# A new opening for a two-layer hybrid decoder: x and the first weights in alternating parts, low-rank sums out unscaled, squares later, and narrow even projections

## The reference, cut to what matters

```python
def rms_norm(x, g, eps=EPS):
    y = x * lax.rsqrt(jnp.mean(x * x, axis=-1, keepdims=True) + eps)
    return y * g

h = rms_norm(x, attn_norm_g[0])          # x: (1, 256, 2048)
p = h @ even_w_in[0]                     # 2048 -> 6304 columns
qa, ka, va = jnp.split(p[..., :3072], 3, axis=-1)
a_out = diff_attention(qa, ka, va, ...)  # 8 heads
b_out = rwkv7_time_mix(p[..., 3072:], ...)  # r, k, v (1024 each), 160 low-rank columns
x = x + concatenate([a_out, b_out]) @ even_w_out[0]
x = x + swiglu(rms_norm(x, ffn_norm_g[0]))
...                                      # layer 1: hgrn2 and its swiglu, then the final norm

# in rwkv7_time_mix: a mix of each token with the one before it, then
xm = p + (prev - p) * mu
w_log = -jax.nn.softplus(-(w0 + jnp.tanh(wl) @ w_up)) - 0.5     # wl, al, gl: the low-rank columns
```

## Time and profile before

| | |
|---|---|
| three runs, median | 2703.5 us (2700.93 to 2703.85) |
| the profiled execution's own time | 2699.04 us |
| its span | 2697.3 us |
| granted clock, mean | 0.991 |
| PE busy | 2589.8 us, 96% |
| DVE busy | 1933.1 us, 72% |
| ACT busy | 1268.1 us, 47% |
| POOL busy | 433.9 us, 16% |
| DMA, mean | 162 GB/s |

### The profile page before, as it was taken

One profiled execution on the slowest core, in us unless ns is written; L12 is line 12 of the kernel. 1 busy time (PEld: TensorE's weight loads), 2 busy tenths in 40 slices (PEclk: granted clock), 3 DMA queues, 4 the chain that ended last, 5 costly groups with the idle time before them and its releaser, 6 DMA issues.

```text
span 2697.3 us, 46875 instructions
## 1 busy us (share of the span) xinstructions
PE 2589.8 (96%) x16654; PEld 2254.0 (84%) x16654; DVE 1933.1 (72%) x2981; ACT 1268.1 (47%) x1721; POOL 433.9 (16%) x426
## 2 busy tenths in 40 slices
PE   7988888889999999999999999998999999999998
PEld 6777777778888888888888888887888888888886
DVE  6676676677666566656698999997666656665666
ACT  5444343445554344434465656564455434433444
POOL 1222222211110011101111212211121001100112
PEclk9999999999999999999999999998999999999999
DMA  6222222225455555555464444443455555555543
GB/s 251 93 99 97 89 96 96 88 87 188 173 188 191 189 188 189 189 187 187 167 205 158 156 158 159 165 156 140 172 189 188 192 187 189 190 189 187 187 164 133
DMA packets 65716, 437.89 MB, mean 162 GB/s; under 512 B 9424, under 2 KB 10832, under 8 KB 16848
## 3 DMA queue, kind: packets, MB, share of 16 engines
q1 hardware_dynamic: 61776, 435.84, 45.4%
q10 hardware_dynamic: 3840, 0.70, 0.1%
HBM read 434.41 MB, written 2.10 MB: 162 GB/s over the span
## 4 chain that ended last, share of the span: by engine, by line
PE 86%; DVE 8%; issue 3%; ACT 2%; DMA 0%; DVEq 0%; ACTq 0%; SPq 0%; POOL 0%; POOLq 0%
PE acc L338 52%; PE acc L343 27%; PE mixer_banks L1555 2%; DVE w_low L307 1%; PE mixer_banks L1272 1%; PE acc L319 1%; ACT w_high L302 1%; PE mixer_banks L1372 1%; PE mixer_banks L1359 1%; ACT arena L638 0%; DVE arena L362 0%; PE mixer_banks L1374 0%; DVE arena L972 0%; DVE arena L960 0%; DVE arena L899 0%
## 5 line engine op out<-in xcount | busy, mean ns | idle before, releaser
L307 DVE TENSOR_TENSOR w_low<-w_raw,w_high 128x1024 fp32r<-128x1024 f32 x838 | 1056.1, 1261 | 417.7 <-ACT w_high L302 407.0
L302 ACT ACTIVATE w_high<-w_raw 128x1024 fp32r<-128x1024 f32 x838 | 883.1, 1059 | 947.0 <-PE acc L343 927.7
L338 PE MATMUL acc<-h_split,w_high 128*128 128x512 f32 x4576 | 1194.9, 398 | 8.5 <-DVE arena L362 8.4
L338 PEld LDWEIGHTS acc<-h_split,w_high 128*128 128x128 f32 x4576 | 817.2, 190 | 161.7 <-issue 18.9
L343 PEld LDWEIGHTS acc<-h_split,w_low 128*128 128x128 f32 x4576 | 642.0, 190 | 55.7
L343 PE MATMUL acc<-h_split,w_low 128*128 128x256 f32 x4576 | 659.7, 282 | 0.0
L464 POOL TENSOR_TENSOR arena<-arena,norm_scale 128x256 f32<-128x256 f32 x202 | 218.6, 1082 | 1787.7 <-DVE arena L362 1786.5
L338 PE MATMUL acc<-mix_split,w_high 128*128 128x512 f32 x1876 | 480.4, 395 | 1.1 <-DVE arena L362 0.6
L338 PEld LDWEIGHTS acc<-mix_split,w_high 128*128 128x128 f32 x1876 | 336.4, 189 | 62.8 <-issue 3.6
L343 PEld LDWEIGHTS acc<-mix_split,w_low 128*128 128x128 f32 x1876 | 260.6, 190 | 21.3
L343 PE MATMUL acc<-mix_split,w_low 128*128 128x256 f32 x1876 | 266.8, 282 | 0.0
(11 more groups left out here) (253 smaller groups left out, 1640.7 us busy)
## 6 DMA issues: line engine op xcount, KB each, us to landing
w_raw<-w_gu SPq DMA_DIRECT2D x176, 1024.0 KB, 4.8
w_raw<-w_down SPq DMA_DIRECT2D x64, 1024.0 KB, 4.9
w_raw<-w_odd SPq DMA_DIRECT2D x64, 1024.0 KB, 4.8
w_raw<-w_even SPq DMA_DIRECT2D x50, 1024.0 KB, 4.9
w_raw<-w_down SPq DMA_DIRECT2D x32, 768.0 KB, 4.2
w_raw<-w_odd_out SPq DMA_DIRECT2D x16, 1024.0 KB, 4.8
w_raw<-w_even_out SPq DMA_DIRECT2D x10, 1024.0 KB, 4.9
w_raw<-w_even_out SPq DMA_DIRECT2D x6, 896.0 KB, 4.5
```

The source lines that it names most:

```text
L302: act.activation(wh[:, self.res, ks], raw[:, self.raw, ks], ACT.Copy).then_inc(high_done, 1)
L307: dve.tensor_tensor(wl[:, self.res, ks], raw[:, self.raw, ks], wh[:, self.res, ks].bitcast(F32), ALU.subtract).then_inc(low_done, 1)
L338: pe.matmul(acc[self.acc][:, 0:2 * T], wh[:, self.res, k], flat(split[:, src(k)]), start=k == 0, stop=k == self.kt - 1)
```

## The change

The diff does these things:

- SyncE loads block 0 in two halves, with the second quarter of x between them.
- ScalarE: quarter 0 of x, first half of block 0, quarter 1, second half, quarters 2 and 3, block 1, half of the squares, block 2, the other half, blocks 3 and 4, then the norm, block 5, and then the low-rank functions. VectorE follows the same order; its squares' tree stands behind block 2 and within block 3.
- The low-rank sums (blocks 0 and 1) leave PSUM unscaled (`raw_sum`), before the norm's scale is known; VectorE scales them later.
- TensorE's norm matmul stands in the middle of block 3, where it stood in the middle of block 1.
- "Narrow": in blocks 0 to 49 `w_high` multiplies the two parts in two matmuls of 256 columns that add up in the same 256 PSUM columns. The evacuation is then one product of those 256 columns with `nrs` on VectorE; GpSimd scales nothing in the even layer, and its consumers wait for `evac_done`.

```diff
-        used[0] = 0
+        used[0] = BEHIND_SHIFTS          # the squares lie behind r3 ... b_sum
         sq_all = take(KT, T)
...
+            def high_products(self, pe, k, both, stop):
+
+                if self.narrow:
+                    for c in range(2):
+                        pe.matmul(acc[self.acc][:, 0:T], wh[:, self.res, k], both[:, c], start=k == 0 and c == 0, stop=False,
+                                  skip_group_check=True)
+                else:
+                    pe.matmul(acc[self.acc][:, 0:2 * T], wh[:, self.res, k], flat(both), start=k == 0, stop=stop)
...
             def evacuate(self, dve, dst):
 
                 self.result(dve)
+                if self.narrow:
+                    dve.tensor_tensor(dst, acc[self.acc][:, 0:T], nrs, ALU.mult).then_inc(evac_done, 1)
+                    return
                 dve.reduce_sum(dst, acc[self.acc].rearrange("p (s t) -> p t s", s=2), AX.X).then_inc(evac_done, 1)
...
-            return lambda u: Block(EVEN + 6 * j + 6 + u, i, 12)
+            return lambda u: Block(EVEN + 6 * j + 6 + u, i, 12, narrow=True)
... SyncE
             load_x(0)
-            Block(LOWRANK).load(sp, w_even[LOWRANK])
-            for q in range(1, 4):
+            sp.wait_ge(low_done, 2)
+            sp.dma_start(raw[:, 0, 0:HALF], w_even[LOWRANK][:, 0:HALF]).then_inc(S["first_half"], 16)
+            load_x(1)
+            sp.dma_start(raw[:, 0, HALF:KT], w_even[LOWRANK][:, HALF:KT]).then_inc(landed[0], 16)
+            for q in range(2, 4):
                 load_x(q)
... GpSimd
-                scale_next(-1)
-                pool.wait_ge(S["even_scaled"], 6 * j + 7)
+                pool.wait_ge(evac_done, 6 * j + 9)
...
-                scale_next(0)
...
-                    if l in (2, 4):
-                        scale_next(l // 2)
...
-                scale_next(3)
-                scale_next(4)
...
-            scale(LOWRANK, r3[:, 0, 1:], "even_scaled")
-            scale(LOWRANK + 1, r3[:, 1, 1:], "even_scaled")
-            for u in range(5):
-                scale(EVEN + u, even_dst[u], "even_scaled")
... ScalarE
-            for half in range(2):
-                Block(LOWRANK).high(act, half)
             for q in range(4):
                 act.wait_ge(S[f"x_in{q}"], 16)
                 for k in range(4 * q, 4 * q + 4):
                     high_part(k, gn[:, G_ATT0 + k:G_ATT0 + k + 1])
+                if q == 0:
+                    act.wait_ge(S["first_half"], 16)
+                    act.activation(wh[:, 0, 0:HALF], raw[:, 0, 0:HALF], ACT.Copy).then_inc(high_done, 1)
+                if q == 1:
+                    Block(LOWRANK).high(act, 1)
...
             for half in range(2):
                 Block(LOWRANK + 1).high(act, half)
-            for q in range(4):
-                act.activation(sq_all[:, 4 * q:4 * q + 4], x[:, 4 * q:4 * q + 4], ACT.Square).then_inc(S["sq"], 4)
+            squares((0, 1))
+            for half in range(2):
+                Block(LOWRANK + 2).high(act, half)
+            squares((2, 3))
+            for n in range(LOWRANK + 3, LOWRANK + 5):
+                for half in range(2):
+                    Block(n).high(act, half)
+            norm(0)
+            for half in range(2):
+                Block(LOWRANK + 5).high(act, half)
... VectorE
+            def raw_sum(n, dst):
+
+                Block(LOWRANK + n, narrow=True).result(dve)
+                dve.tensor_scalar(dst, acc[n][:, 0:T], 1.0, None, ALU.mult).then_inc(evac_done, 1)
...
+            for half in range(2):
+                Block(LOWRANK + 1).low(dve, half)
+            raw_sum(0, r3[:, low_home[0], 1:])
+            for half in range(2):
+                Block(LOWRANK + 2).low(dve, half)
+            raw_sum(1, r3[:, low_home[1], 1:])
             dve.wait_ge(S["sq"], KT)
             dve.tensor_tensor(sq_all[:, 0:8], sq_all[:, 0:8], sq_all[:, 8:16], ALU.add).then_inc(S["sq_sum"], 8)
+            Block(LOWRANK + 3).low(dve, 0)
...
+            Block(LOWRANK + 3).low(dve, 1)
+            for half in range(2):
+                Block(LOWRANK + 4).low(dve, half)
...
+            dve.wait_ge(S["norm_rstd"], 1)
+            Block(EVEN, narrow=True).evacuate(dve, even_dst[0])
...
+            for n in range(2):
+                home = r3[:, low_home[n]]
+                dve.tensor_tensor(home[:, 1:], home[:, 1:], nrs, ALU.mult).then_inc(S["dve_once"], 1)
+                dve.wait_ge(S["dve_once"], 2 * n + 3)
+                dve.tensor_tensor(d3[:, n], home[:, 0:T], home[:, 1:], ALU.subtract).then_inc(S["dve_once"], 1)
+                dve.wait_ge(S["dve_once"], 2 * n + 4)
+                dve.scalar_tensor_tensor(xm[:, n], d3[:, n], gn[:, G_MUW + n:G_MUW + n + 1], home[:, 1:],
+                                         ALU.mult, ALU.add).then_inc(S["low_mixed"], 1)
+            Block(EVEN + 1, narrow=True).evacuate(dve, even_dst[1])
... TensorE
-            norm(0)
-            for n in range(LOWRANK + 2, EVEN + 6):
-                for half in range(2):
-                    Block(n).products(pe, half, hs)
+            for k in range(KT):
+                pe.wait_ge(S["h_low"], k + 1)
+                Block(LOWRANK, narrow=True).tile(pe, k, hs)
+            for n in range(LOWRANK + 1, EVEN + 6):
+                Block(n, narrow=True).products(pe, 0, hs)
+                if n == LOWRANK + 3:
+                    pe.wait_ge(S["sq_sum"], KT + 1)
+                    pe.matmul(bank(0)[:, 0:T], ones, nss, start=True, stop=True).then_inc(S["sq_total"], 1)
+                Block(n, narrow=True).products(pe, 1, hs)
...
-                pe.wait_ge(S["even_scaled"], 6 * j + 7)
+                pe.wait_ge(evac_done, 6 * j + 9)
                 pe.matmul(bank(3), rot, flat(aqk), start=True, stop=True).then_inc(S["at_rot"], 1)
```

More of the change, by code:

```diff
@@ L141, in build @@
         b_sum = take(2, P + 1)
+        BEHIND_SHIFTS = used[0]
         e1 = take(2, P + 1)
@@ L281, in build, with __init__ @@
         class Block:
-            def __init__(self, base, i=None, step=0, kt=KT):
-                self.kt = kt
+            def __init__(self, base, i=None, step=0, kt=KT, narrow=False):
+                self.kt, self.narrow = kt, narrow
                 self.n = base if i is None else base + step * i
@@ L318, in tile @@
                 stop = k == self.kt - 1
-                pe.matmul(acc[self.acc][:, 0:2 * T], wh[:, self.res, k], flat(split[:, k]), start=k == 0, stop=stop)
+                self.high_products(pe, k, split[:, k], stop)
                 last = pe.matmul(acc[self.acc][:, 0:T], wl[:, self.res, k], split[:, k, 0], start=False, stop=stop,
@@ L337, in run @@
                 for k in ks:
-                    pe.matmul(acc[self.acc][:, 0:2 * T], wh[:, self.res, k], flat(split[:, src(k)]), start=k == 0, stop=k == self.kt - 1)
+                    self.high_products(pe, k, split[:, src(k)], k == self.kt - 1)
                 if begins:
@@ L565, in _, with squares @@
                     high_part(k, gn[:, G_ATT0 + k:G_ATT0 + k + 1])
+                if q == 0:
[3 more added lines that the diff above has]
+                    Block(LOWRANK).high(act, 1)
+            def squares(qs):
+                for q in qs:
+                    act.activation(sq_all[:, 4 * q:4 * q + 4], x[:, 4 * q:4 * q + 4], ACT.Square).then_inc(S["sq"], 4)
             for half in range(2):
                 Block(LOWRANK + 1).high(act, half)
-            for q in range(4):
-                act.activation(sq_all[:, 4 * q:4 * q + 4], x[:, 4 * q:4 * q + 4], ACT.Square).then_inc(S["sq"], 4)
+            squares((0, 1))
[8 more added lines that the diff above has]
+                Block(LOWRANK + 5).high(act, half)
             act.wait_ge(S["lam_dve"], 3)
             act.activation(lamt[:, 2:4], lamt[:, 0:2], ACT.Exp).then_inc(S["lam_act"], 1)
-            for half in range(2):
-                Block(LOWRANK + 2).high(act, half)
-            norm(0)
-            for half in range(2):
-                Block(LOWRANK + 3).high(act, half)
             act.wait_ge(S["low_mixed"], 2)
@@ L687, in even_step @@
                     act.dma_start(pln, par_ln[j + 1]).then_inc(S["rw_late"], 16)
-            for u in range(5):
+            for u in range(2, 5):
                 for half in range(2):
@@ L827, in _ @@
             dve.wait_ge(S["gains_in"], 16)
-            for half in range(2):
-                Block(LOWRANK).low(dve, half)
-            for k in range(KT):
-                dve.wait_ge(S["h_high"], k + 1)
-                low_part(k, gn[:, G_ATT0 + k:G_ATT0 + k + 1])
+            def raw_sum(n, dst):
+                Block(LOWRANK + n, narrow=True).result(dve)
+                dve.tensor_scalar(dst, acc[n][:, 0:T], 1.0, None, ALU.mult).then_inc(evac_done, 1)
+            low_home = (2, 1)
+            for q in range(4):
+                for k in range(4 * q, 4 * q + 4):
+                    dve.wait_ge(S["h_high"], k + 1)
+                    low_part(k, gn[:, G_ATT0 + k:G_ATT0 + k + 1])
+                if q < 2:
```

(12 more changed lines are left out.)

29 lines of the change are left out of this document (10 added, 19 removed).

## The result

| | before | changed |
|---|---|---|
| median of four runs | 2702.82 us (2700.93 to 2703.85) | 2680.37 us (2677.95 to 2682.93) |
| profiled execution, span | 2699.04, 2697.3 us | 2677.95, 2676.2 us |
| DVE busy | 1933.1 us | 1908.0 us |
| POOL busy | 433.9 us | 373.4 us |
| first matmul of the first even step | 67.6 us | 59.9 us |

The ratio of the times is 0.9919, 95% interval 0.9903 to 0.9934: 22 us faster, where 12 were forecast and 2684 was the low end of the range. The direction was right, the size was not. A second set of five runs of the changed kernel gave 2681.28 us and 0.9931 (0.9918 to 0.9945).

A forecast was written before the change was run, and what follows sets the result against it. It took PE, 86% of the chain, as the bound, with DVE's chain setting each even step's first part. Opening -9.9 and steps -2.3 give -12.2 us, from 2703.5 to a median of 2691.3; 8-in-10 range 2684 to 2699.

The forecast's parts named there:

- The opening: Before the first even step: no PE stop, no lower clock behind it, earlier block 1, less narrow-tile cost; 9.9 us saved.
- block 0's term: In the opening: PE starts at 9.7 us, block 0 ends at 16.9, so block 1 starts 3.3 us earlier, at 17.1.
- The tight places: In the opening: margins of 1.1 us before the matmul with ones and 0.4 us at block 2's evacuation for block 4.
- The steps: Even steps: shorter evacuations and less GpSimd contention against dearer narrow tiles; 0.25 us less per step, 2.3 in all.
- PE's cap: First part of a step: PE's own work lets only 0.7 of DVE's 1.0 us chain gain through.
- The hop over GpSimd ahead of line 1305: Even steps: removed semaphore hop in front of PE's matmul, said to stand beside DVE's chain; costed at nothing.
- (A): Opening gives only 5.5 to 8 us, being short of data, and steps nothing; 2696 us, chance 0.17.
- (B): Opening as forecast, but in the steps PE pays every narrow tile and DVE's gain is absorbed; 2699.5 us, chance 0.13.
- (C): Loading each weight tile twice is not hidden between mixer matmuls, so the kernel is slower; up to 2719 us, chance 0.05.
- (D): Late squares' tree or scale brings stop and lower clock back in block 3 or 4; half the opening's gain, 2698, chance 0.07.

The follow-up runs named there:

- the one with wide steps: Changed kernel with all even-step blocks wide, evacuated by reduce_sum and a product with the scale on DVE, GpSimd scaling nothing; 2693.82 us, ratio 0.9976 to before.
- the squares' experiment: Changed kernel with all four squares and their tree ahead of block 2's conversions, the matmul with ones back in block 1; 2689.13 us, ratio 0.9948 to before.

## Why the prediction was wrong

**The opening** was right in mechanism: no stop before the matmul with ones, full clock from block 1 on, narrow tiles 10 to 11 ns dearer (2.88 against 2.79 us for half a block, 0.17 us a block where 0.14 was forecast; the prediction's own 2 x 120 - 230 is 10, not 9). It gave 7.7 instead of 9.9 us, because block 0's term was mis-sized: the first half landed at 8.05 us, not 7.5, PE began at 10.62, not 9.7, and its tiles kept the pace of the lower clock (0.64 us a tile against 0.36) up to about 15.8, though the windows give a granted clock of 1.00 there, 5 us instead of the 3 I took; block 0 ended at 18.7, not 16.9. That is 1.6 of the 2.2 us by the start of block 1 (18.7, not 17.1). From there to the first step it took 41.2 us, not 40.7; the dearer tiles (0.2) and a short wait for an evacuation at 48.1 (0.17 us idle) are most of that. The tight places held: that wait was PE's only one between 18.7 and 59.9, and the matmul with ones came at 33.1, behind the forecast 31 to 32, without a stop.

**The steps** failed at one sentence: "Three such operations run slow there beside one scaling and the two cosine products that stay; without the scaling the cosine products start earlier and one of the three runs free: 0.5 us." The cosine products do start earlier, but by 12.7 us: their own inputs are ready before the step begins, and only the scaling ahead of them in GpSimd's program had held them. All three DVE operations run free, 0.96 us falling to 0.42 each, 1.62 us a step. I had the diff's line, the wait for `6 * j + 9`, and did not ask when that count is reached. The experiment that puts the wait back to the sixth block brings two of the three back to 0.96 us and 0.6 us to the step; the one that swaps the order in the old kernel frees two of three and takes 0.6 us off. Against the 0.5 us forecast for this term stand 1.62 freed and 0.34 lost again at the head.

**PE's cap**, "I take 0.7 of the 1.0", was wrong as well. It rested on the wait of 0.5 us at line 1319. In the changed kernel the counterpart of that matmul group has no wait at all, and the first part still comes out 1.5 us shorter (33.5 against 35.0). DVE does not need that group's result until after the sine product, the sum, an evacuation and a `low` part; an engine that waits at a place does not bound the chain that passes by it.

The sum of a steady step, redone with measured durations: three operations freed -1.62; two evacuations at 0.42 instead of 0.69, -0.54; line 1083 at 0.94 instead of 0.60, +0.34; the pause behind line 1085, 0.51 instead of 0.16, +0.35; the second part, 32.45 from PE's last wait on instead of 32.07, +0.38. That is -1.1, and -1.2 was measured. The hop over GpSimd ahead of line 1305, where PE had waited 0.5 us for the scaling and which the prediction cost at nothing, is not in this sum, and at most 0.1 us is left for it. The first two steps gave more. The first has no operations at its head: without their two terms the sum is -1.8, and -1.8 was measured. In the second the head's operation took 0.42 where it had taken 0.69, and no pause stood behind line 1085 in either kernel: -2.1 by the sum, measured -2.3. GpSimd's products ran beside that operation too, and the trace shows why it stayed fast. It began first, at 123.26 us, and the second product 0.02 us behind it:

```profile
123.26 0.42 DVE L1083 TENSOR_TENSOR arena<-arena 128x256 f32<-128x256 f32 x1 [0.51 <-ACT arena L696]
123.28 0.98 POOL L495 TENSOR_TENSOR arena<-arena,constants_sb 128x256 f32<-128x256 f32 x1
```

In the third step the product was ahead by 0.06 us (line 1083 from 188.08), and it was DVE that waited:

```profile
188.02 0.72 POOL L495 TENSOR_TENSOR arena<-arena,constants_sb 128x256 f32<-128x256 f32 x1
```

**Rivals.** (A) is half true: 7.7 us lies in its range, and part of its reason, the lower clock over block 0, was seen; its second half, steps that give nothing, was wrong. (B) is refuted: PE pays its narrow tiles in the second part (+0.38 us), but DVE's gain is not absorbed. (C) is refuted: 2.88 us for 24 matmuls is 120 ns each, a second load of the same tile costs nothing over the first, and between the mixer's matmuls, where (C) put its cost, the second part grew by 0.38 us only. (D) did not occur in the change, and the squares' experiment shows that its mechanism is real at 8.4 us (its forecast of 2698 left the steps' 2.3 us out).

**The stalls** of DVE's loop, of which I had said that no edit touches them, were between 3.3 and 4.7 us in all kernels but the one with wide steps, where DVE stood still for 6.2; they were 8.9 us in sum before and 7.3 in the changed one. What sets them stays open; 1.6 us of the result is theirs.

## What to carry to other kernels

When an operation is removed from an in-order engine, replay what stood behind it: its inputs may have been ready long ago, and it moves not by the removed duration but to the place of its own last input. On a chain of DVE operations, an operation with two SBUF inputs that begins under a GpSimd product ends only behind it, so ask which of the two begins first, and place such products by a wait where DVE reads PSUM, is idle or has just begun a long operation. An idle gap on another engine caps a gain only if the chain needs that engine's result there.

## What the runs showed of the hardware

A DVE operation (tensor_tensor) of 128x256 with two SBUF inputs takes 0.42 us alone. Begun while a GpSimd product runs, it ends 0.27 to 0.29 us after that product: so it was for all 148 in the twelve traces used here that began 0.15 us or more ahead of the product's end. In before, product and operation ended at 200.17 and 200.45 us (line 1050, 0.60 us long), 211.03 and 211.30 (line 927, 0.96); in the changed kernel at 188.74 and 189.02 (line 1083, 0.94). So the 0.54 us is no fixed price but what was left of the product. The 162 operations that read PSUM and began under a product kept their 0.41 to 0.42. It goes both ways, and who begins first has the way: the GpSimd product took 1.50 us when it began behind a DVE `low` part (1.22 us, unchanged) and 0.73 at its shortest in that kernel, and in the first 620 us of before the four `low` parts that began behind a product took 1.34 to 1.76. The Trainium skill ("SBUF — State Buffer", Who interferes with whom) calls the port pair that the two engines share an exclusive lock and lets the order of issue decide who blocks. The traces agree, by the 0.28 us behind the product's end on the one side and the 0.42 us of line 1083 in the second step on the other.

Where DVE's loop begins again, twice in each kernel, DVE stands still for 3.3 to 6.2 us, waiting for nothing that the profile shows; DVE has no such idle time at the same place in the other steps. The other engines run dry behind it, and the granted clock falls to 0.50 for some 6 us:

```profile
259.00:262.00 3.00, 0.00 (x0) 0.00 (x0) 1.63 (x4) 0.73 (x1) 0.00 (x0) 0.93 0.01 3
262.00:265.00 3.00, 1.73 (x6) 1.45 (x7) 2.97 (x9) 1.33 (x4) 0.00 (x0) 0.50 0.01 3
265.00:268.00 3.00, 3.00 (x16) 3.00 (x16) 2.93 (x7) 2.59 (x7) 0.00 (x0) 0.50 0.00 0
```

These are windows of the changed kernel's fourth step. PE idles through the first of them and runs at half its clock through the next two.
